# Attention scores kept negated, and the group sums of a Mamba-2 layer issued by matmul form

## The chip, the cores and the metric

The kernel runs on one core of one Trainium2 chip. The metric is the device time of one launch in microseconds (us), the median of several runs. The kernel before was run three times: 1904.80, 1904.31 and 1900.27 us, median 1904.31 us.

## The reference, cut to what matters

One inference step of a small encoder for two request groups that share weights: 512 prompt tokens and 64 sample tokens, 576 token columns in all (`TOK`), everything in fp32. Layer 0 mixes tokens by windowed attention with sinks, layer 1 by a Mamba-2 recurrence (SSD); both also attend to 256 memory tokens and are followed by a squared-ReLU MLP. The change touches two places:

```
def sink_probs(scores, sink):
    m = jnp.maximum(jnp.max(scores, axis=-1, keepdims=True), sink)
    p = jnp.exp(scores - m)
    return p / (jnp.sum(p, axis=-1, keepdims=True) + jnp.exp(sink - m))

# swa_prompt, swa_sample: scores are q.k / 8 + bias, bias = -slope * |distance|
# ssm_mixer, at its end: RMSNorm over each of 8 groups of 192 channels
y = rmsnorm(y.reshape(b, l, SSM_GROUPS, SSM_INNER // SSM_GROUPS), norm_w.reshape(SSM_GROUPS, SSM_INNER // SSM_GROUPS))
```

## The kernel before, in words

Five engines run five instruction streams, tied by semaphores. All large projections stream their weights from HBM as slabs of 128 output features (128 x 1024 floats, 512 KB). A slab passes through SP (load into `raw`, L2139), ACT (`w_hi`, the part that TensorE's fp32r format holds exactly, L471), POOL (`w_lo` = `raw` - `w_hi`, L1941) and TensorE (`eighth`, L917: for each of 8 feature tiles `w_hi`, `w_lo` and `w_hi` again times `big_hi`, `big_hi` and `big_lo`, each in two halves of 288 columns). A ring of four slabs (`RING`) lets the loads run ahead. An eighth is 6 matmul instructions.

**Attention (layer 0).** 24 heads are taken in 12 query tiles of two heads. A tile has five units u0 to u4: u0 the sample's tokens, u1/u2 and u3/u4 the two heads of two pairs of prompt blocks. `attention_steps()` writes out one list of steps that every engine walks: S (scores, PE L1041/L1052), B (`bias_max`, DVE), E (`exps`, ACT), N (`normalise`, DVE), T (transposes on PE, L1065 to L1070, and the copy to `p_t` on ACT, L627 to L631), V (values, PE L1081), O (`take_out`, DVE L1418), K (an eighth of the next query projection on PE) and Q (end of its slab: DVE's L1527/L1529, ACT's `w_hi`). PE fills its time between attention steps with the 8 K of a tile.

`bias_max` (L1554) reads the scores from PSUM, adds the bias, writes `prob` and, through its accumulator, the row maximum with the sink as its start (`stat[..., 0]`), one instruction per head or block, with an accumulator read behind each. It then waits for its own semaphore `biased` and negates the maxima into `stat[..., 1]` with a small `tensor_scalar` (L1561), which signals `max_done`. ACT's `exps` waits for `max_done`, and computes exp(`prob` - max) with the negated maximum as its bias (L610) and exp(sink - max) (L614, L617). SP's loads of the bias table (L2183) for the tile after next wait for `biased`, and the next slab's load stands behind them in SP's queue.

**SSD (layer 1).** Eight groups are taken in four turns of two groups (`PAIRS`; a turn is one pass of `turn`, driven by `ssd_steps`). Each turn runs K eighths of the next tiles' projections between the steps A, seg, off, st, diag, acc for five blocks; near its end come Q (gate with `zs`, DVE L1905; squares `gsq`, ACT L827), G and N. G sums the squares over each group's 192 channels: 1.5 tiles of 128 partitions, so that for group m and column half h one full-height matmul (contraction over 128 rows, L1338) and one half-height matmul (64 rows, L1339; rows 0 to 63 for m = 0, rows 64 to 127 for m = 1) with a matrix of ones accumulate into PSUM bank 4 + 2m + h. ACT's G then takes ln and exp of all four banks (L832, L835), and DVE's N multiplies `mix` by the result (L1911). The last 10 eighths of a turn stand behind G on PE, except that the steps walk on with N between them; the next turn begins with 16 more eighths. Behind its G part ACT has a table load and the next tile's tanh (L779), for which DVE's `silu` (L1791) waits; DVE's `slab_end` (L1418, L1769, L1784) makes the next tiles, and POOL copies their tails (L2042) and then makes a `w_lo`. `alone(pe)` (L449) is a semaphore increment on a semaphore that nobody waits for.

The code quoted above the printed functions is all that the words can't say:

```
BLOCKS = 5; UNITS_J = 5; TILES = 12; RING = 4; KT = 8
fill(eighths - 10); steps.append(("G", 0)); fill(eighths - 6); steps.append(("N", 0)); fill(eighths)
```

## Time and profile before

| what | value |
|---|---|
| runs | 1904.80, 1904.31, 1900.27 us; median 1904.31 us |
| the profiled execution, its own time | 1899.76 us |
| its span in the trace | 1898.0 us, 31359 instructions |
| granted TensorE clock over the span | 0.992 of full speed |
| busy share: PE, PE loads, DVE, ACT, POOL | 95%, 90%, 45%, 34%, 42% |
| HBM traffic | 76 GB/s over the span |

The profile is of one execution. "PE" is TensorE's matmuls, "PEld" its weight loads, which overlap matmuls. An fp32 matmul shows as two entries of PE and two of PEld, an fp32r one as one. A "wait" is idle time of an engine before an instruction, put down to whatever ended last before it; "issue" is idle time that no other instruction explains. The chain of waits is followed back from the last instruction. The attention stage lies between 134 and 303 us of the span, the four turns between 942 and 1317 us.

### The profile page before, as it was taken

What the parts mean: (1) busy time and instruction counts of PE and PEld (TensorE: products, weight loads), DVE (VectorE), ACT (ScalarE), POOL (GpSimd) and SP (SyncE); (2) the same over time, 40 slices, a digit from 0 to 9 for tenths busy, and PEclk for the clock granted to TensorE, in tenths of its full rate; (3) what the DMA queues carried; (4) which work ended last, traced back from release to release, by engine and by line L of the source; (5) the groups of instructions that cost most, each with busy time, mean ns of one, the idle gap of its engine ahead of it and who ended that gap; (6) DMA issues with size and microseconds to landing.
All of it is one profiled execution on the core that took longest, in us unless ns stands there. A gap on an engine that the chain in (4) does not pass through costs nothing.

```text
span 1898.0 us, 31359 instructions
## 1 busy us (share of the span) xinstructions
PE 1799.6 (95%) x13177; PEld 1705.3 (90%) x13177; DVE 853.1 (45%) x1649; ACT 640.7 (34%) x1148; POOL 793.1 (42%) x478
## 2 busy tenths in 40 slices
PE   6998998999999999998999999998999999999996
PEld 6997876998999999998888888787799899999996
DVE  6337887316312121138867676764613611212124
ACT  6326665325222121225323342332623412222221
POOL 1331210333646363541465665755133645545451
PEclk9999999999999999999899999999999999999998
DMA  6521110221222222221212111112022222222221
GB/s 230 181 67 57 62 62 30 67 90 65 81 79 84 83 79 89 78 88 61 67 38 66 59 54 60 45 65 99 23 84 73 72 85 78 90 78 87 80 79 72
DMA packets 42076, 146.57 MB, mean 77 GB/s; under 512 B 4816, under 2 KB 6480, under 8 KB 41680
## 3 DMA queue, kind: packets, MB, share of 16 engines
q1 hardware_dynamic: 40144, 140.59, 21.8%
q10 hardware_dynamic: 1792, 3.97, 0.6%
q8 instruction: 105, 1.72, 0.4%
q14 instruction: 35, 0.29, 0.0%
HBM read 138.13 MB, written 6.41 MB: 76 GB/s over the span
## 4 chain that ended last, share of the span: by engine, by line
PE 79%; DVE 13%; issue 3%; ACT 3%; POOL 1%; DMA 1%; SPq 0%; DVEq 0%; ACTq 0%; POOLq 0%
PE ps L917 66%; DVE u L1784 3%; PE ps L1287 1%; DVE mix L1427 1%; PE ps L900 1%; DVE x L1430 1%; PE ps L1052 1%; PE ps L1070 1%; DVE xp L1418 1%; PE ps L1156 1%; DVE prob L1554 1%; PE ps L1133 1%; DVE big_lo L1371 1%; DMA raw<-in_slabs 1%; PE ps L1081 1%
## 5 line engine op out<-in xcount | busy, mean ns | idle before, releaser
L1941 POOL TENSOR_TENSOR w_lo<-raw,w_hi 128x1024 fp32r<-128x1024 f32 x225 | 555.7, 2472 | 751.1 <-ACT w_hi L471 658.9
L917 PE MATMUL ps<-big_hi,w_hi 128*128 128x288 f32 x3552 | 786.4, 302 | 11.0 <-POOL w_lo L1941 3.1
L917 PE MATMUL ps<-big_hi,w_lo 128*128 128x288 f32 x3552 | 767.0, 297 | 0.0
L917 PE MATMUL ps<-big_lo,w_hi 128*128 128x288 f32 x3552 | 759.7, 297 | 7.5 <-DVE big_lo L1371 7.5
L917 PEld LDWEIGHTS ps<-big_hi,w_hi 128*128 128x128 f32 x3552 | 574.7, 189 | 22.5 <-issue 16.3
L917 PEld LDWEIGHTS ps<-big_lo,w_hi 128*128 128x128 f32 x3552 | 571.9, 189 | 12.8 <-DVE big_lo L1371 11.9
L917 PEld LDWEIGHTS ps<-big_hi,w_lo 128*128 128x128 f32 x3552 | 576.0, 189 | 0.1
L471 ACT ACTIVATE w_hi<-raw 128x1024 fp32r<-128x1024 f32 x242 | 255.2, 1056 | 480.1 <-DMA raw<-in_slabs 479.9
L1683 DVE TENSOR_TENSOR mix<-ps,mix 128x576 f32<-128x576 f32 x62 | 46.9, 757 | 306.3 <-PE ps L917 306.3
L1671 DVE SCALAR_TENSOR_TENSOR relu<-ps,rstd 128x576 f32<-128x576 f32 x60 | 45.4, 756 | 280.2 <-PE ps L917 280.2
L1984 POOL TENSOR_TENSOR hid<-relu 128x576 f32<-128x576 f32 x64 | 98.7, 1544 | 158.7 <-DVE relu L1671 158.5
L1784 DVE SCALAR_TENSOR_TENSOR u<-xp,cpar,u 128x579 f32<-128x579 f32 x84 | 108.6, 1293 | 8.4 <-ACT u L765 6.4
L713 ACT ACTIVATE big_hi<-relu 128x576 fp32r<-128x576 f32 x64 | 43.9, 686 | 157.1 <-DVE relu L1671 155.5
L1369 DVE TENSOR_TENSOR big_lo<-hid,big_hi 128x576 fp32r<-128x576 f32 x64 | 75.6, 1181 | 11.1 <-POOL hid L1984 11.1
L1407 DVE TENSOR_TENSOR sq_sum<-sq_sum,sq 128x576 f32<-128x576 f32 x20 | 16.2, 809 | 114.1 <-ACT sq L490 113.8
L2042 POOL COPY tails<-xp 128x3 f32<-128x3 f32 x56 | 16.0, 315 | 102.3 <-DVE xp L1769 97.1
L821 ACT ACTIVATE dec<-ps 128x384 f32<-128x384 f32 (+1 forms) x40 | 16.1, 455 | 121.1 <-PE ps L1287 121.1
L610 ACT ACTIVATE prob<-prob,stat 128x256 f32<-128x256 f32 (+2 forms) x108 | 50.5, 470 | 9.9 <-DVE stat L1561 9.8
L1554 DVE CUSTOM_DVE_ANT_0 prob<-ps,bias,par 128x128 f32<-128x128 f32 (+2 forms) x120 | 49.2, 440 | 8.2 <-PE ps L1052 7.9
L1418 DVE TENSOR_SCALAR mix<-ps 128x384 f32<-128x384 f32 (+5 forms) x62 | 33.4, 539 | 43.0 <-PE ps L1325 19.0
L917 PE MATMUL ps<-m_hi,w_hi 128*128 128x256 f32 x128 | 38.6, 302 | 14.2 <-POOL w_lo L1941 10.9
L1874 DVE TENSOR_TENSOR dec<-dec,cbm 128x768 f32<-128x768 f32 (+1 forms) x20 | 28.2, 1411 | 51.7 <-ACT dec L821 51.7
(200 smaller groups left out, 1744.8 us busy)
## 6 DMA issues: line engine op xcount, KB each, us to landing
raw<-in_slabs SPq DMA_DIRECT2D x242, 512.0 KB, 3.4
bias<-in_alibi SPq DMA_DIRECT2D x12, 256.0 KB, 2.7
x<-in_x SPq DMA_DIRECT2D x2, 1152.0 KB, 8.3
out_h<-state ACTq DMA_DIRECT2D x4, 384.0 KB, 2.6
out_y<-x SPq DMA_DIRECT2D x2, 576.0 KB, 2.8
kms<-in_mk SPq DMA_DIRECT2D x2, 512.0 KB, 5.1
vms<-in_mv SPq DMA_DIRECT2D x2, 512.0 KB, 6.1
out_y<-x SPq DMA_DIRECT2D x1, 864.0 KB, 3.5
```

The source lines that it names most:

```text
L471: act.activation(w_hi[:, s % RING], raw[:, s % RING], ACT.Copy).then_inc(hi_done, 1)
L610: act.activation(ap, ap, ACT.Exp, bias=stat[:, r, 1, b:b + 1], accum_out=stat[:, r, 2, b:b + 1])
L713: act.activation(big_hi[:, m], relu[:, m % 2], ACT.Square).then_inc(act_hi, 1)
L917: ins = pe.matmul(ps[:, bank + h, 0:hi_c - lo_c], w[:, s % RING, kt], a[:, k0 + kt, lo_c:hi_c], start=start, stop=stop, skip_group_check=True)
L1369: ins = dve.tensor_tensor(dst, src, hi.bitcast(F32), ALU.subtract)
L1418: return dve.tensor_scalar(dst, src, 1.0, None, ALU.mult)
L1554: ins = dve.tensor_tensor_reduce(prob[half, r, k, c0:c1], ps[half, bank, k * 2 * P + c0:k * 2 * P + c1], bias[half, j, e, c0 + d:c1 + d], 1.0,
L1671: dve.scalar_tensor_tensor(out=halves(relu[:, m % 2]), in0=src, scalar=0.0, in1=halves(rstd[:, 1]), op0=ALU.max, op1=ALU.mult).then_inc(fr ...
L1683: dve.tensor_tensor(halves(mix[:, m]), src, halves(mix[:, m]), ALU.add).then_inc(freed, 1)
L1784: dve.scalar_tensor_tensor(out=u[:, t], in0=xp[:, t % 2, j:j + UC], scalar=cpar[:, t, j:j + 1], in1=u[:, t], op0=ALU.mult, op1=ALU.add).th ...
L1941: pool.tensor_tensor(w_lo[:, s % RING], raw[:, s % RING], w_hi[:, s % RING].bitcast(F32), ALU.subtract).then_inc(lo_done, 1)
L1984: pool.tensor_tensor(hid[:, m % 2], relu[:, m % 2], relu[:, m % 2], ALU.mult).then_inc(hid_done, 1)
```

## The change

The attention scores are stored negated: `tensor_tensor_reduce` now has a factor of -1.0 and takes the minimum, started from a negated sink (`minus_sink`, made once by a `tensor_scalar` of 24 columns before the first query tile). The minimum is already the negated maximum, so L1561 and DVE's wait before it go, ACT waits for `biased` instead of `max_done`, and its exponentials take `scale=-1.0` on `prob` and none on `stat`. The memory attention keeps `max_done`, whose count is now `UNITS` lower. In G the four full-height matmuls are issued first, then the four half-height ones with the row half alternating; one `alone(pe)` stands in front of all instead of four. Functions and lines after the edit are one to four lines further down (L917 is L918, L1554 is L1558).

```diff
--- before.py
+++ after.py
@@ -253,6 +253,7 @@
         par = main.take("par", [P, N_PAR])
         mats = main.take("mats", [P, 4, P])
         eps = main.take("eps", [P, 1])
+        minus_sink = main.take("minus_sink", [P, 2 * TILES])
 
         main.p = (main.p + 31) // 32 * 32
         big_start = main.p
@@ -601,20 +602,20 @@
 
                 n_, q, u = n.n + t, t // UNITS_J, t % UNITS_J
                 r, sink = n_ % 4, C_SINK + 2 * q + (u - 1) % 2
-                act.wait_ge(max_done, n_ + 1)
+                act.wait_ge(biased, n_ + 1)
                 if u == 0:
                     parts = [(0, prob[:, r, 0, 0:DEC + P])]
                 else:
                     parts = [(b, prob[:, r, b, P if u < 3 and b == 0 else 0:2 * P]) for b in range(2)]
                 for b, ap in parts:
-                    act.activation(ap, ap, ACT.Exp, bias=stat[:, r, 1, b:b + 1], accum_out=stat[:, r, 2, b:b + 1])
+                    act.activation(ap, ap, ACT.Exp, bias=stat[:, r, 0, b:b + 1], scale=-1.0, accum_out=stat[:, r, 2, b:b + 1])
                 if u == 0:
                     for e in range(2):
                         half = slice(e * DEC, (e + 1) * DEC)
-                        ins = act.activation(stat[half, r, 3, 0:1], stat[half, r, 0, 0:1], ACT.Exp, scale=-1.0,
+                        ins = act.activation(stat[half, r, 3, 0:1], stat[half, r, 0, 0:1], ACT.Exp,
                                              bias=par[half, C_SINK + 2 * q + e:C_SINK + 2 * q + e + 1])
                 else:
-                    ins = act.activation(stat[:, r, 3, :], stat[:, r, 0, :], ACT.Exp, scale=-1.0, bias=par[:, sink:sink + 1])
+                    ins = act.activation(stat[:, r, 3, :], stat[:, r, 0, :], ACT.Exp, bias=par[:, sink:sink + 1])
                 ins.then_inc(exp_done, 1)
 
             def copy_t(t):
@@ -649,7 +650,7 @@
 
                 def exps(c):
                     n_, u = n.n + c, c % 3
-                    act.wait_ge(max_done, n_ + 1)
+                    act.wait_ge(max_done, n_ + 1 - UNITS)
                     rows = P if u else DEC
                     for b in range(2 if u else 1):
                         ins = act.activation(prob[0:rows, n_ % 4, b], ps[0:rows, S_BANK + n_ % 2, b * N_MEM:(b + 1) * N_MEM],
@@ -1329,14 +1330,16 @@
                         pe.wait_ge(gsq_done, at(loop, gsq_done, 1))
                         pe.wait_ge(state_done, at(loop, state_done, BLOCKS))
 
+                        alone(pe)
                         for m in range(2):
                             for h in range(2):
-                                c0, c1 = h * HALF, (h + 1) * HALF
-                                o = ps[:, 4 + 2 * m + h, 0:HALF]
-                                r0 = m * HD
-                                alone(pe)
-                                pe.matmul(o, mats[:, 1], gsq[:, 2 * m, c0:c1], start=True, stop=False)
-                                ins = pe.matmul(o, mats[r0:r0 + HD, 1], gsq[r0:r0 + HD, 1, c0:c1], start=False, stop=True)
+                                pe.matmul(ps[:, 4 + 2 * m + h, 0:HALF], mats[:, 1], gsq[:, 2 * m, h * HALF:(h + 1) * HALF],
+                                          start=True, stop=False)
+                        for h in range(2):
+                            for m in range(2):
+                                half = slice(m * HD, (m + 1) * HD)
+                                ins = pe.matmul(ps[:, 4 + 2 * m + h, 0:HALF], mats[half, 1], gsq[half, 1, h * HALF:(h + 1) * HALF],
+                                                start=False, stop=True)
                         ins.then_inc(gsum_done, 1)
 
             loop.per = SSM_PER
@@ -1530,6 +1533,7 @@
                                          in1=halves(rstd[:, 1]), op0=ALU.mult, op1=ALU.mult).then_inc(freed, 1)
 
             dve.wait_ge(stored, 16 * 4)
+            dve.tensor_scalar(minus_sink[:], par[:, C_SINK:C_SINK + 2 * TILES], -1.0, None, ALU.mult)
             own.mark(dve.memset(q_s[:], 0.0))
             own.wait(loop)
             for j in range(QT):
@@ -1550,15 +1554,12 @@
                         half, e, k, c0, c1, d = slice(b * DEC, (b + 1) * DEC), b, 0, 0, P + DEC, b * DEC
                     else:
                         half, e, k, c0, c1, d = slice(0, P), (u - 1) % 2, b, P if u < 3 and b == 0 else 0, 2 * P, 0
-                    sink = C_SINK + 2 * q + e
+                    sink = 2 * q + e
                     ins = dve.tensor_tensor_reduce(prob[half, r, k, c0:c1], ps[half, bank, k * 2 * P + c0:k * 2 * P + c1],
-                                                   bias[half, j, e, c0 + d:c1 + d], 1.0,
-                                                   par[half, sink:sink + 1], ALU.add, ALU.max,
+                                                   bias[half, j, e, c0 + d:c1 + d], -1.0,
+                                                   minus_sink[half, sink:sink + 1], ALU.add, ALU.min,
                                                    stat[half, r, 0, k:k + 1])
                 ins.then_inc(biased, 1)
-                sums = 2 if u else 1
-                dve.wait_ge(biased, n_ + 1)
-                dve.tensor_scalar(stat[:, r, 1, 0:sums], stat[:, r, 0, 0:sums], -1.0, None, ALU.mult).then_inc(max_done, 1)
 
             def normalise(n_, rows, parts, sink=True, sums=2):
 
```

On PE the order of G's eight matmuls moves in each of the four turns. Before (`ps` the PSUM banks, `gsq` the squares, `mats` the ones; L917 are the eighths around it; a full-height one is L1338, a half-height one L1339):

```order
L917 MATMUL ps<-big_lo,w_hi 128x288 x2
L1338 MATMUL ps<-gsq,mats 128x288
L1339 MATMUL ps<-gsq,mats 128x288
L1338 MATMUL ps<-gsq,mats 128x288
L1339 MATMUL ps<-gsq,mats 128x288
L1338 MATMUL ps<-gsq,mats 128x288
L1339 MATMUL ps<-gsq,mats 128x288
L1338 MATMUL ps<-gsq,mats 128x288
L1339 MATMUL ps<-gsq,mats 128x288
L917 MATMUL ps<-big_hi,w_hi 128x288 x2
```

And in the change:

```order
L918 MATMUL ps<-big_lo,w_hi 128x288 x2
L1336 MATMUL ps<-gsq,mats 128x288 x4
L1341 MATMUL ps<-gsq,mats 128x288 x4
L918 MATMUL ps<-big_hi,w_hi 128x288 x2
```

The same eight matmuls stand between the same neighbours, with one change of form between them instead of seven.

On DVE the piece around units u1 and u2 of a tile, between the normalisation of u0 and the copy of finished values; before:

```order
L1575 TENSOR_SCALAR prob<-prob,stat 128x192 [waits dve_self]
L1554 ISA prob,stat<-ps,bias,par 128x128 [waits t_done,s_done]
L1554 ISA stat 128x1
L1554 ISA prob,stat<-ps,bias,par 128x256
L1554 ISA stat 128x1
L1561 TENSOR_SCALAR stat<-stat 128x2 [waits biased]
L1554 ISA prob,stat<-ps,bias,par 128x128 [waits t_done,s_done]
L1554 ISA stat 128x1
L1554 ISA prob,stat<-ps,bias,par 128x256
L1554 ISA stat 128x1
```

And in the change:

```order
L1576 TENSOR_SCALAR prob<-prob,stat 128x192 [waits dve_self]
L1558 ISA prob,stat<-ps,bias,minus_sink 128x128 [waits t_done,s_done]
L1558 ISA stat 128x1
L1558 ISA prob,stat<-ps,bias,minus_sink 128x256
L1558 ISA stat 128x1
L1558 ISA prob,stat<-ps,bias,minus_sink 128x128 [waits t_done,s_done]
L1558 ISA stat 128x1
L1558 ISA prob,stat<-ps,bias,minus_sink 128x256
L1558 ISA stat 128x1
L1421 TENSOR_SCALAR mix<-ps 128x512 [waits v_done]
```

Nothing stands between the two units any more, and behind them comes the copy out of PSUM, then the normalisation of u1.

## Rows read from the trace of the kernel before

**Rows 1.** Busy time by stage: attention, turns (us; PE, PEld, DVE, ACT, POOL; clock)

```profile
134.00:303.00 169.00, 157.95 (x1295) 130.94 (x1294) 140.14 (x579) 107.83 (x370) 26.08 (x11) 1.00 0.15 54
942.00:1317.00 375.00, 352.27 (x2488) 313.35 (x2486) 250.62 (x341) 125.89 (x183) 222.14 (x189) 1.00 0.18 60
```

**Rows 2.** Page, the chain that ended last, share of the span by engine

```profile
PE 79%; DVE 13%; issue 3%; ACT 3%; POOL 1%; DMA 1%; SPq 0%; DVEq 0%; ACTq 0%; POOLq 0%
```

**Rows 3.** Waits of PE from 134 to 303 us: total us, times, longest

```profile
PE ps L1065 <- DVE prob L1575: 4.0, 3, 1.8
PE ps L1070 <- DVE prob L1575: 3.5, 7, 1.1
PE ps L1070 <- ACT p_t L631: 2.1, 2, 1.1
PE ps L1052 <- DVE stat L1554: 1.4, 4, 0.5
```

**Rows 4.** The negation and the biased maximum by line (ns min/median/max)

```profile
L1561 DVE TENSOR_SCALAR stat<-stat x60: 153/170/1981, 135.0 to 299.2; 128x2 f32<-128x2 f32 x48, 128x1 f32<-128x1 f32 x12
L1554 DVE CUSTOM_DVE_ANT_0 prob<-ps,bias,par x120: 337/476/485, 134.1 to 298.7; 128x256 f32<-128x256 f32 x72, 64x192 f32<-64x192 f32 x24, 128x128 f32<-128x128 f32 x24
```

**Rows 5.** Timeline, sixth query tile (start, us, engine, line, operation, count, idle before)

```profile
205.99 0.32 DVE L1575 TENSOR_SCALAR prob<-prob,stat 128x192 f32<-128x192 f32 x1
...
207.46 2.38 POOL L1941 TENSOR_TENSOR w_lo<-raw,w_hi 128x1024 fp32r<-128x1024 f32 x1 [11.22 <-ACT w_hi L471]
...
208.14 1.71 DVE L1561 TENSOR_SCALAR stat<-stat 128x2 f32<-128x2 f32 x1
...
210.58 1.13 PE L1052 MATMUL ps<-k_all,q_t 64*128 64x256 f32 x8 [0.28 <-DVE stat L1554]
```

**Rows 6.** Timeline, first query tile: ACT behind the slab load

```profile
146.89 1.06 ACT L471 ACTIVATE w_hi<-raw 128x1024 fp32r<-128x1024 f32 x1 [2.20 <-DMA raw<-in_slabs]
```

**Rows 7.** Timeline, eleventh query tile

```profile
274.81 2.34 POOL L1941 TENSOR_TENSOR w_lo<-raw,w_hi 128x1024 fp32r<-128x1024 f32 x1 [10.72 <-ACT w_hi L471]
274.84 2.44 DVE L1575 TENSOR_SCALAR prob<-prob,stat 128x192 f32<-128x192 f32 x1
```

**Rows 8.** Timeline of PE's loads through G of the first turn

```profile
1022.26 0.30 PEld L1338 LDWEIGHTS ps<-gsq,mats 128*128 128x128 f32 x2 [0.16 <-issue]
...
1022.94 0.29 PEld L1339 LDWEIGHTS ps<-gsq,mats 64*128 64x128 f32 x2 [0.39 <-issue]
...
1027.71 0.30 PEld L917 LDWEIGHTS ps<-big_hi,w_hi 128*128 128x128 f32 x2 [0.38 <-issue]
```

**Rows 9.** Chain of waits, 462 to 466 us: four full-height fp32 matmuls in a row

```profile
463.67 1.95 PE ps L869 x8
```

**Rows 10.** Timeline of PE, memory attention: two full-height matmuls of 256 columns

```profile
1327.27 1.13 PE L1133 MATMUL ps<-km,mix 128*128 128x256 f32 x4
```

**Rows 11.** Timelines of ACT, DVE, POOL and PE behind G, first turn

```profile
1027.82 1.23 ACT L832 ACTIVATE grs<-ps,eps 128x1152 f32<-128x1152 f32 x1 [2.09 <-PE ps L1339]
...
1023.70 2.44 DVE L1791 SCALAR_TENSOR_TENSOR u<-th,u 128x579 f32<-128x579 f32 x1 [2.56 <-ACT th L779]
...
1029.76 0.17 DVE L1418 TENSOR_SCALAR xp<-cpar 128x3 f32<-128x3 f32 x1 [1.17 <-PE ps L917]
...
1033.22 1.07 DVE L1791 SCALAR_TENSOR_TENSOR u<-th,u 128x579 f32<-128x579 f32 x1 [2.50 <-ACT th L779]
...
1031.27 2.41 POOL L1941 TENSOR_TENSOR w_lo<-raw,w_hi 128x1024 fp32r<-128x1024 f32 x1
...
1051.26 0.50 PE L917 MATMUL ps<-big_hi,w_hi 128*128 128x288 f32 x2 [1.57 <-DVE zs L1775]
```

**Rows 12.** Third turn: a piece of the chain, and DVE's first tiles of the next

```profile
1236.11 21.00 PE ps L917 x156
...
1256.35 1.55 DVE L1775 SCALAR_TENSOR_TENSOR zs<-ps,rstd 128x576 f32<-128x576 f32 x2 [0.18 <-DVE skips L1418]
```

**Rows 13.** Timeline of ACT, last turn

```profile
1316.07 1.22 ACT L832 ACTIVATE grs<-ps,eps 128x1152 f32<-128x1152 f32 x1 [3.92 <-PE ps L1339]
```

## The prediction

> **What bounds the kernel now.** I read the busy times by stage first. In both stages that the change touches PE is busy 94% of the time: 157.95 of 169.00 us in attention, 352.27 of 375.00 us in the turns, at the full clock (1.00, the 2.4 GHz level) [rows 1]. The chain that ended last runs 79% through PE and 13% through DVE [rows 2]. So an edit pays where it shortens PE's own stream or a piece where PE stands still, and a saving on DVE or ACT alone pays nothing. A whole-span share doesn't say which, so I took the two places apart.
>
> In attention PE stands still for 169.0 - 157.95 = 11.05 us, and the table of waits accounts for all of it: 4.0 + 3.5 + 2.1 + 1.4 = 11.0 us [rows 3]. That is the ceiling for the first half of the change, whatever DVE saves.
>
> In the turns the matmuls of G are themselves on PE's stream. The loads show the cost of their order: after the first full-height matmul the load of the half-height one comes 0.68 us later and only after 0.39 us of idle time that nothing explains but "issue"; the whole of G lasts from 1022.26 to 1027.71, 5.45 us for eight matmuls, 0.68 us each [rows 8].
>
> **Part 1, the negation.** It removes 60 instructions of L1561 and 60 waits of DVE for its own semaphore, and adds one `tensor_scalar` of 24 columns long before PE's first wait of the stage; that one is covered by the projections and costs nothing (uncovered, some 0.2 us by the median of L1561). The -1.0 factor and the minimum ride in an instruction that exists; ACT's `scale` likewise. I take both at nothing: the same instruction with other constants. The bounds are 0 and, if a minimum cost one L1561's median more per use, 120 x 0.17 us of DVE, most of it beside PE.
>
> The median negation takes 0.170 us [rows 4]; with the wait in front I count 0.2 us per unit, on DVE and, for the first `exps` behind it, on ACT. That is 12 us of DVE, nearly all beside a busy PE. What matters more is the longest, 1.98 us. In the sixth tile POOL's `w_lo` runs from 207.46 to 209.84; the negation starts at 208.14 and takes 1.71 us, to 209.85: it is held until POOL is done. L1554 reads scores from PSUM and is never held, its longest of 120 is 0.485 us [rows 4, 5]. So the second unit's L1554 comes after 209.85, and PE's next scores (L1052, 210.58) wait 0.28 us for it [rows 5]. Without L1561 the two units follow each other and end some 1.6 us earlier, and the wait is gone. Term by term, on PE:
> - L1052 waiting for L1554, four times, 1.4 us [rows 3]: gone, 1.4 us.
> - L1070 waiting for L1575, seven times, 3.5 us [rows 3]. Two of about 1.1 us come behind the copy of a query tile, which itself waits for PE; they stay. Five small ones share 3.5 - 2.2 = 1.3 us. Each is the end of a string B, negation, N on DVE; 0.2 us less each, and the whole in two that follow a held negation: 1.2 us.
> - L1070 waiting for ACT's `p_t`, twice, 2.1 us. `p_t` stands on ACT behind a `w_hi` that waits 2.20 us for its slab [rows 3, 6]; that load stands on SP behind a bias load which waits for `biased` of u4. That comes 0.2 us earlier by one negation: 0.4 us for two.
> - L1065 waiting for L1575, three times, 4.0 us: two (longest 1.8 us) where L1575 itself is held, 2.44 us at 274.84 against a `w_lo` that began at 274.81 [rows 3, 7]. Nothing of the change stands in front of either by more than a tenth of a us, they stay. The third is the stage's first unit: 0.2 us.
>
> Sum 3.2 us, between 0 and 11.
>
> **Part 2, the group sums.** PE issues the same eight matmuls with two changes of form (into and out of the half-height run) in place of eight. A full-height fp32 matmul of 288 columns among its like takes 1.95 / 4 = 0.49 us [rows 9], so a change of form costs 0.68 - 0.49 = 0.19 us. For the half-height ones on alternating row halves: four such of 256 columns (L1052, eight entries) take 1.13 us [rows 5], as much as two full-height ones of 256 columns (L1133, four entries, 1.13 us [rows 10]). So a pair costs what one full-height matmul costs. G becomes 4 x 0.49 + 0.19 + 2 x 0.49 + 0.19 = 3.32 us, 2.13 us less a turn. The removed `alone` increments I take at nothing: the idle time before a full-height load (with one in front) is the same 0.38 to 0.39 us as before a half-height one (without) [rows 8]; bounds 0 and 3 x 0.19 us.
>
> One rule of the Trainium skill speaks against the first four: "TensorE: Matmul & The Clock Gate", Part 3, says that a weight load overlaps a running matmul only when its row group differs. By it the eight loads of the full-height run, 0.15 us each by the 0.30 us of two [rows 8], would come on top, 1.2 us a turn, and G would take 4.5 us. The four in a row of [rows 9] show no such gaps, and the measurement decides.
>
> What a turn gains depends on who is late next.
> - Turns 1 and 2: ACT waits 2.09 us for the sums [rows 11], so ln, exp and the next tanh come up to 2.1 us earlier. But DVE can start its next tile (1029.76) only 1.17 us earlier, when it is free; POOL's `w_lo` (1031.27) follows that tile's tails and moves by the same 1.17 us; and L1791 (1033.22), now ready early, falls under it as its predecessor did at 1023.70 (2.44 us against some 0.75 us unheld). DVE thus gains 1.17 us, and PE, which waits 1.57 us for DVE's first `zs` tile at 1051.26, gains as much [rows 11]: 1.17 us a turn, the rest turns into a longer wait there.
> - Turn 3: the chain runs 21.0 us through PE behind G, with no wait at all, and DVE's first `zs` tile is done (half of 1.55 us after 1256.35) at about 1257.1, as PE ends its eighths and goes on to A's transposes [rows 12]. Between 1.17 and 2.13 us, near the latter since PE is first: 2.0 us.
> - Turn 4: ACT has been free for 3.92 us when the sums come, and N and the memory attention stand behind it [rows 13]: 2.1 us.
>
> Sum 2 x 1.17 + 2.0 + 2.1 = 6.4 us, between 3 and 8.5.
>
> **Total**: 3.2 + 6.4 = 9.6 us, 0.50%. The profiled execution took 1899.76 us (span 1898.0), 4.55 us under the median of 1904.31; against itself the sum gives 1890.2, against the median 1894.7 us. Behind each stage PE runs on without waits that depend on the saved work, so the gain is kept. I forecast **1894.7 us**.
>
> **Rivals.**
> - *The half-height pairs don't overlap.* For it: L1339 alone takes 0.68 us as L1338 does. Against: L1052 against L1133. G is then 8 x 0.49 + 2 x 0.19 = 4.3 us, 1.15 us less a turn; turns 1 and 2 keep about 1.15. Total 3.2 + 4.6 = 7.8: 1896.5 us. Chance 0.12.
> - *The hold moves to the next instruction of DVE.* The instruction held now is not special: L1575 is held in the last tiles. If N of u1 starts before POOL ends (209.84), DVE is freed as late as now, and the 1.4 us and half of the 1.2 us stay. Against it: between them stands a copy of 0.7 us, and N needs exponentials of more than a us that can't start before 209. Then 1.2 + 6.4 = 7.6: 1896.7 us. Chance 0.15. The Trainium skill, "SBUF — State Buffer", who interferes with whom, has this rule: the later of a GpSimd instruction and a VectorE one with two SBUF inputs or in a two-port mode is blocked until the first ends. By it the copy out of PSUM is free and N is not.
> - *The two held L1575 slip in front of POOL.* At 274.84 against 274.81 the race is lost by 0.03 us; a tenth of a us on DVE might win it. Two times 1.7 us more: 13.0 in all, 1891.3 us. Chance 0.15.
> - *The turns absorb it.* DVE, already the last at 1051.26, gives nothing: 3.2 + 0 + 0 + 2 + 2: 1897.1 us. Chance 0.07.
> - *Slower.* In the sixth tile L1575 of u0 ends at 206.31, 1.15 us before POOL's `w_lo` [rows 5]; in the eleventh it loses that race and PE stands 1.7 us. If ACT, relieved of waits, makes `w_hi` over a us earlier in tiles 4 to 10, seven tiles pay 1.74 us each, 12.2 us, and gain nothing of the 3.2 but 1.2: -6.4 - 1.2 + 12.2 = +4.6, 1908.9 us. Against: `w_hi` stands on ACT behind `p_t` copies whose time PE sets. It decides from about 1.1 us of shift. Chance 0.03.
>
> **How the numbers follow.** Forecast 0.48, the rivals as given. A measurement of this kernel can tell about 0.3%, 5.7 us. The runs before spread over 4.5 us, which adds to every case: the range 1886.5 to 1901.5 us takes in the best case less the spread below the median, and above it half of each part's gain failing (1899.5) and a little of the spread. Faster by over 0.3%: most of the forecast, two thirds of the smaller ones, 0.78; within 0.3% 0.18; slower 0.04.
>
> **What would show it.** L1561 gone and no entry of DVE over 1 us in tiles 4 to 10; PE's idle time in the attention stage down from 11.0 to about 8 us, L1052's waits gone; G at 3.3 us, with idle loads only at its two changes of form; ACT's ln in turns 1 and 2 without a wait worth naming; the wait for `zs` in turns 1 and 2 up from 1.57 to about 2.5 us. G at 4.3 us refutes the pairing, an L1575 or `tensor_tensor` of 1 to 2 us in the middle tiles refutes the end of the hold, and a first wait of the next turn that grows by the full 2.1 us would mean the turns absorb it.

## The result, and the profile after

The changed kernel ran in 1888.85 us (median of 5 runs, 1883.80 to 1890.73) against 1903.85 us for the kernel before on the same chip (5 runs, 1900.27 to 1904.80): ratio 0.9923, 95% interval 0.9905 to 0.9941, 15.0 us less where 9.6 were forecast. The profiled execution took 1888.85 us, its span 1887.0 us (before: 1899.76 and 1898.0).

Two single executions differ in more than the change, so I first matched PE's streams: the same matmul in both traces, and by how much it comes earlier. Between 132.7 and 299 us (times of before) the distance grows by 3.9 us, through the four turns by 7.4 us. The rest is not work of the edited lines: the trace after is 2.1 us late at the start of the K projection, where its granted clock stayed at the lower level longer, and wins 1.4 us behind 1356 us, where the clock of the one before fell to it for some 3 us and that of this one did not. Another 0.3 us come between the two stages. -3.9 - 7.4 - 1.4 - 0.3 + 2.1 = -10.9 of the 11.0 us.

Busy time by stage, the two stages of [rows 1] (PE, PEld, DVE, ACT, POOL, clock):

```profile
134.00:300.00 166.00, 157.60 (x1300) 131.17 (x1299) 123.67 (x521) 106.23 (x370) 27.72 (x12) 1.00 0.16 55
935.00:1308.00 373.00, 348.13 (x2528) 316.60 (x2528) 256.18 (x344) 127.18 (x185) 223.10 (x190) 1.00 0.18 61
```

PE's idle time in attention fell from 11.05 to 8.4 us. Its table of waits, to be held against [rows 3] (all lines are one to four higher now: L1554 is L1558, L1575 is L1576, L1052 is L1053):

```profile
PE ps L1066 <- DVE prob L1576: 3.9, 3, 1.8
PE ps L1071 <- DVE prob L1576: 2.2, 2, 1.1
PE ps L1071 <- ACT p_t L632: 2.0, 2, 1.1
```

The row of scores waiting for the biased maximum is gone, as are the five small waits of L1071, and no entry of DVE in tiles 4 to 10 lasts over 1 us. The held normalisation of the eleventh tile stands, [rows 7]:

```profile
273.29 2.50 DVE L1576 TENSOR_SCALAR prob<-prob,stat 128x192 f32<-128x192 f32 x1
273.33 2.34 POOL L1942 TENSOR_TENSOR w_lo<-raw,w_hi 128x1024 fp32r<-128x1024 f32 x1 [10.25 <-ACT w_hi L472]
```

DVE is now first by 0.04 us, where it had been second by 0.03, and is held all the same: 2.50 us where an unheld one takes 0.32 [rows 5]. The trace before had shown this already, in the twelfth tile:

```profile
289.96 2.50 DVE L1575 TENSOR_SCALAR prob<-prob,stat 128x192 f32<-128x192 f32 x1
290.00 2.35 POOL L1941 TENSOR_TENSOR w_lo<-raw,w_hi 128x1024 fp32r<-128x1024 f32 x1 [12.84 <-ACT w_hi L471]
```

In all the traces of this case this normalisation starts 0.03 to 0.04 us ahead of `w_lo` 19 times, and it is held each time. The profile gives GpSimd's times only roughly, so which of the two is truly first can't be told.

G in the third turn, from the chain of waits; 3.35 us in place of 5.45 [rows 8], and the same 21 us of PE behind it as in [rows 12]:

```profile
1225.51 2.18 PE ps L1336 x8
1227.69 1.17 PE ps L1341 x8
1228.86 20.98 PE ps L918 x156
```

Behind G of the first turn, timelines of ACT, DVE and PE; they answer to [rows 11]:

```profile
1023.61 1.23 ACT L833 ACTIVATE grs<-ps,eps 128x1152 f32<-128x1152 f32 x1
...
1044.32 2.33 DVE L1421 TENSOR_SCALAR skips<-par 128x6 f32<-128x6 f32 x1
1046.83 1.42 DVE L1776 SCALAR_TENSOR_TENSOR zs<-ps,rstd 128x576 f32<-128x576 f32 x2 [0.18 <-DVE skips L1421]
...
1047.74 0.50 PE L918 MATMUL ps<-big_hi,w_hi 128*128 128x288 f32 x2 [2.34 <-DVE zs L1776]
```

ACT finds the sums ready (it waited 2.09 us for them), and PE now waits 2.34 us for the first `zs` where it waited 1.57: of the 2.1 us that G became shorter, 0.8 went into this wait. A tiny instruction stands in front of that `zs`: `skips`, 6 elements, takes 2.33 us beside a `w_lo` that began at 1044.25.

### The profile page after: what moved, and what is told of

The parts are those of the page before. It is cut to its first block, busy times and chain, and to the rows that moved or that the text cites. A ratio compares the mean times of both kernels' runs of the same rounds, so it can differ in the third digit from the quotient of the medians.

```text
span 1887.0 us, 31288 instructions
## 1 busy us (share of the span) xinstructions
PE 1788.9 (95%) x13177; PEld 1702.6 (90%) x13177; DVE 837.0 (44%) x1590; ACT 639.2 (34%) x1148; POOL 791.9 (42%) x478
## 4 chain that ended last, share of the span: by engine, by line
PE 78%; DVE 13%; ACT 4%; issue 3%; POOL 1%; DMA 1%; SPq 0%; DVEq 0%; ACTq 0%; POOLq 0%
PE ps L918 66%; DVE u L1785 3%; PE ps L1288 1%; DVE mix L1430 1%; PE ps L901 1%; PE ps L1082 1%; PE ps L1053 1%; DVE x L1433 1%; PE ps L1071 1%; DVE xp L1421 1%; PE ps L1157 1%; PE ps L1134 1%; DVE big_lo L1374 1%; DMA raw<-in_slabs 1%; ACT u L766 1%
## 5 line engine op out<-in xcount | busy, mean ns | idle before, releaser
L918 PE MATMUL ps<-big_hi,w_hi 128*128 128x288 f32 x3552 | 783.6, 301 | 12.5 <-DVE zs L1776 4.7
L918 PE MATMUL ps<-big_lo,w_hi 128*128 128x288 f32 x3552 | 757.1, 297 | 7.7 <-DVE big_lo L1374 7.7
L918 PE MATMUL ps<-big_hi,w_lo 128*128 128x288 f32 x3552 | 763.3, 296 | 0.0
L918 PEld LDWEIGHTS ps<-big_hi,w_hi 128*128 128x128 f32 x3552 | 573.0, 189 | 24.1 <-issue 17.8
L918 PEld LDWEIGHTS ps<-big_lo,w_hi 128*128 128x128 f32 x3552 | 569.4, 189 | 13.1 <-DVE big_lo L1374 12.1
L918 PEld LDWEIGHTS ps<-big_hi,w_lo 128*128 128x128 f32 x3552 | 573.8, 189 | 0.1
L1558 DVE CUSTOM_DVE_ANT_0 prob<-ps,bias,minus_sink 128x128 f32<-128x128 f32 (+2 forms) x120 | 48.4, 440 | 13.7 <-PE ps L1053 11.8
L918 PE MATMUL ps<-m_hi,w_hi 128*128 128x256 f32 x128 | 39.7, 310 | 14.4 <-POOL w_lo L1942 11.1
```

What stands on the lines that cost most here:

```text
L918: ins = pe.matmul(ps[:, bank + h, 0:hi_c - lo_c], w[:, s % RING, kt], a[:, k0 + kt, lo_c:hi_c], start=start, stop=stop, skip_group_check=True)
L1558: ins = dve.tensor_tensor_reduce(prob[half, r, k, c0:c1], ps[half, bank, k * 2 * P + c0:k * 2 * P + c1], bias[half, j, e, c0 + d:c1 + d], ...
```

## The experiments

Twelve kernels ran. Every one carries a profile; those with several runs also a ratio to the kernel before on the same chip.

### neg_only and sums_only: each half alone

`neg_only` is the changed kernel with G's loop as in the diff's removed lines; `sums_only` is the kernel before with the added ones.

> The changed kernel with the matmuls of G in their old order: the negation's half alone. If the two halves add as in the prediction, the attention stage is as in the changed kernel: PE's entries from the stage's start to its end in 3.9 us less than before, no entry of DVE over 1 us in tiles 4 to 10, and G lasts its old 5.45 us in each turn, so 3 to 5 us less than before in all (ratio 0.997 to 0.9985). Rival: the turns also gained by the negation (max_done is no longer raised there, the waits are other ones); then G is 5.45 us and the turns still come out over 1 us shorter than before.

> The kernel before with G's matmuls in the new order: the second half alone. Theory: G lasts 3.3 us in place of 5.45, turns 1 and 2 gain 1.5 us each, turn 3 2.2, turn 4 2.1, 7.4 us in all (ratio about 0.996), and the attention stage keeps its 11 us of PE idle time and L1561 its hold of 1.7 to 2.0 us. Rival: part of the 15 us between the medians stands in neither half but in how the two fall together; then neg_only and sums_only gain clearly less in sum than the changed kernel does.

`neg_only`: 1890.84 us (6 runs, 1884.31 to 1896.81), ratio 0.9939 (0.9918 to 0.9960). `sums_only`: 1895.66 us (5 runs), ratio 0.9964 (0.9951 to 0.9977). The traces say what the theory says: `neg_only` gains 4.0 us in attention, its waits there are those of the changed kernel, and G keeps its old pace (two rows of the chain, one matmul each):

```profile
1226.24 0.71 PE ps L1339 x2
1226.95 0.68 PE ps L1340 x2
```

Its four turns still gain 0.4 us together. That is not the negation: `before_shifted` below, the kernel before with nothing but its tiles moved, has the same turns.

The time of `neg_only` does not agree: 11 us less, where its trace accounts for 4.4 in the two places. And its six runs lie in two clumps, 1884.3 to 1887.3 and 1894.4 to 1896.8. Its profile is one of the quick ones, and the matched streams show where: between 1488 and 1879 us, in one unbroken stretch of PE without a wait in it, it gains 9.5 us. That is taken up below.

`sums_only` shows the second surprise. I read how long each turn lasts from one G to the next, by the start of G's first matmul in PE's timelines (before: 1022.29, 1126.46, 1230.62 and 1310.62 us):

| kernel | turn 1 | turn 2 | turn 3 | wait for `zs` in turns 1 and 2 |
|---|---|---|---|---|
| before | 104.17 | 104.16 | 80.00 | 1.6 |
| neg_only | 104.04 | 104.05 | 79.88 | 1.6 |
| changed | 102.69 | 102.66 | 77.81 | 2.3 |
| sums_only | 104.38 | 102.76 | 77.90 | 2.3 |
| same_half | 102.66 | 104.28 | 77.79 | 2.3 |
| before_shifted | 104.05 | 104.06 | 79.90 | 1.6 |
| after_unshifted | 104.36 | 102.77 | 77.90 | 2.3 |

The column "turn 1" lasts from the first G to the second. Of turns 1 and 2 each gains 1.4 to 1.5 us or nothing, with the same waits. Where the tiles lie as in the kernel before (`sums_only`, `after_unshifted`) it is 1.4 us; the other 0.1 us comes with the moved tiles alone. The windows of `sums_only` behind its wait for `zs` (the number before the last two is the granted clock):

```profile
1052.00:1054.00 2.00, 0.09 (x1) 0.12 (x2) 1.82 (x3) 0.20 (x1) 1.62 (x2) 1.00 0.60 223
1054.00:1056.00 2.00, 2.00 (x11) 1.98 (x12) 1.71 (x4) 1.43 (x3) 0.94 (x2) 0.64 0.03 8
1056.00:1058.00 2.00, 2.00 (x11) 2.00 (x10) 0.75 (x2) 0.89 (x2) 2.00 (x3) 0.50 0.00 0
```

and the same place in the changed kernel:

```profile
1046.00:1048.00 2.00, 0.26 (x2) 0.29 (x3) 1.82 (x3) 0.38 (x1) 1.44 (x2) 1.00 0.56 219
1048.00:1050.00 2.00, 2.00 (x19) 2.00 (x18) 1.74 (x5) 1.46 (x4) 1.11 (x2) 1.00 0.00 0
1050.00:1052.00 2.00, 2.00 (x19) 2.00 (x18) 0.96 (x4) 1.27 (x3) 2.00 (x3) 1.00 0.03 8
```

PE stood still as long in both; in one execution the clock then fell to the 1.2 GHz level for some 3 us, 11 matmuls in 2 us in place of 19, and the turn's gain was gone (a turn with the fall is 1.6 us longer than one without).

### same_half: is it the alternation?

```
-                        for h in range(2):
-                            for m in range(2):
+                        for m in range(2):
+                            for h in range(2):
                                 half = slice(m * HD, (m + 1) * HD)
```

> The changed kernel with the four half-height matmuls of G in the order h inside m, so that two in a row use the same half of the rows. If alternating halves are what lets two of them overlap, the half-height run takes 4 x 0.49 us in place of 2 x 0.49 for its starts, and G about 4.3 us in place of 3.35, 0.7 to 1.0 us more a turn. If not (a half-height matmul is cheap as such, or only the changes of form cost), G stays at 3.3 to 3.4 us.

One run, 1885.01 us (its last stretch is a quick one too, by 9.5 us). G from its chain:

```profile
1228.46 2.17 PE ps L1336 x8
1230.62 1.18 PE ps L1341 x8
```

3.35 us again, to the hundredth: the order in which the row halves are issued does nothing. That does not say that the pairs don't overlap. The eight entries of the half-height run don't start one after the other in either kernel, but two at a time. A window of a tenth of a us shows the first pair, and in the changed kernel I add the second:

```profile
1227.62 0.51 PE L1341 MATMUL ps<-gsq,mats 64*128 64x288 f32 x2
1227.96 0.41 PE L1341 MATMUL ps<-gsq,mats 64*128 64x288 f32 x2
```

and in `same_half`:

```profile
1230.55 0.52 PE L1341 MATMUL ps<-gsq,mats 64*128 64x288 f32 x2
```

The two starts of a pair lie 0.01 us apart, four pairs in a row, in both orders. In the kernel before nothing starts in pairs, each entry comes 0.34 us behind the one before it:

```profile
1230.94 0.41 PE L1338 MATMUL ps<-gsq,mats 128*128 128x288 f32 x1
1231.28 0.51 PE L1339 MATMUL ps<-gsq,mats 64*128 64x288 f32 x1
```

Are half-height matmuls cheap as such? The kernel before has a place that answers: L1308 of a turn's first block runs two half-height matmuls in a row, both on rows 0 to 63, and two full-height ones of the same 192 columns in the next block:

```profile
960.18 0.91 PE L1308 MATMUL ps<-sq,btok 64*128 64x192 f32 x4
970.51 0.81 PE L1308 MATMUL ps<-sq,btok 128*128 128x192 f32 x4
```

From entry to entry it is 0.16 us in both, with no pairs; the 0.1 us more is the first step behind a change of form. So a half-height matmul costs what a full-height one costs when its neighbours use the same rows, and half of that when they use the other rows. In `same_half` the pairs must then be one of each half, out of the order of issue; the trace doesn't name the rows of an entry, so this last step is argued.

### old_order_one_alone: the increments

```
+                        alone(pe)
                         for m in range(2):
                             for h in range(2):
                                 c0, c1 = h * HALF, (h + 1) * HALF
                                 o = ps[:, 4 + 2 * m + h, 0:HALF]
                                 r0 = m * HD
-                                alone(pe)
                                 pe.matmul(o, mats[:, 1], gsq[:, 2 * m, c0:c1], start=True, stop=False)
```

The other lines are the changed kernel's, with the matmuls interleaved as before.

> The matmuls of G interleaved as in the kernel before, with one increment of alone(pe) in front of the eight in place of four. If the changes of form are the cost, G stays at 5.4 to 5.5 us and the turns are as long as before. If the increments cost something, G is shorter: by up to 3 x 0.19 = 0.57 us (4.9 us), which would leave that much less to the order.

One run, 1895.45 us. Entries of 0.68 us as in the kernel before, and the same G of 5.4 us:

```profile
1227.79 0.68 PE ps L1340 x2
1228.47 0.68 PE ps L1339 x2
```

The three increments cost nothing. By PE's timelines G takes 5.42 us from its first matmul to the next eighth here and before, and 3.28 to 3.29 us in the first three turns of every kernel with the new order, 2.14 us less. The steps from one entry's start to the next say where they come from. Among full-height entries a step is 0.24 us, two to a matmul, as in [rows 9]. Around a change of form two steps are 0.34 us, the one into the new form and the one behind it: 0.19 to 0.20 us for a change. From pair to pair of the half-height run it is again 0.24 to 0.25 us. Six changes less at 0.19 are 1.1 us, and four half-height matmuls that share their time two by two are 2 x 0.49 = 1.0 us less than four that stand alone. Together that is the 2.1 us, and it fits both totals: 8 x 0.49 + 8 x 0.19 = 5.44, and 6 x 0.49 + 2 x 0.19 = 3.32.

### neg_kept_unread and neg_by_column: DVE's hold, DVE's string, or ACT

```
                 ins.then_inc(biased, 1)
+                sums = 2 if u else 1
+                dve.wait_ge(biased, n_ + 1)
+                dve.tensor_scalar(stat[:, r, 1, 0:sums], stat[:, r, 0, 0:sums], -1.0, None, ALU.mult)
```

That is `neg_kept_unread`, on top of the changed kernel. `neg_by_column` is the kernel before with

```
-                dve.tensor_scalar(stat[:, r, 1, 0:sums], stat[:, r, 0, 0:sums], -1.0, None, ALU.mult).then_inc(max_done, 1)
+                for k in range(sums):
+                    ins = dve.tensor_scalar(stat[:, r, 1, k:k + 1], stat[:, r, 0, k:k + 1], -1.0, None, ALU.mult)
+                ins.then_inc(max_done, 1)
```

> The changed kernel with the negation and the wait in front of it put back on DVE, while ACT goes on reading the negated maxima of the first instruction, so that the result of the added one is read by nobody. It parts DVE's time from ACT's. If the gain of the attention stage comes from DVE no longer standing behind POOL's w_lo, the added instruction is held for 1.7 to 2.0 us in tiles 4 to 10 again, PE's waits for it are back (1.4 us of L1053 <- DVE) and the stage is 2 to 3.9 us longer than in the changed kernel (165.1 us from the stage's start in the changed kernel's trace against 169.0 before). Rival: the gain is ACT's shorter wait (exps a negation earlier); then the stage keeps at least 3 of its 3.9 us although the instruction is back. From the other clock drops and the last stretch's rate of an execution, neither reads anything; the stage alone is compared.

> The kernel before with the negation of two maxima written as two instructions of one column each (96 more instructions would be 108 in place of 60). In the kernel before every held negation had two columns, and none of the 12 with one column fell beside a w_lo, so the trace does not tell whether the form matters. If it is the two-column form that is held behind POOL, none of the single-column ones takes over 0.3 us, the waits of L1052 for L1554 (1.4 us) go and attention is 1 to 2.5 us shorter than before, with an L1575 or tensor_tensor no more held than in the changed kernel. If any instruction of DVE between two SBUF operands is held, the first of the two takes 1.7 us as before and attention is as long as before or up to 0.5 us longer. The Trainium skill, "VectorE: DVE Perf Modes", says that a single-source instruction takes the mode with both port pairs when its outermost dimension over one is even or equal in source and result; a row of one element has no such dimension, so by it the first case is to be expected.

The instruction whose result nobody reads, by its line, and PE's waits in attention (one run, 1893.99 us):

```profile
L1565 DVE TENSOR_SCALAR stat<-stat x60: 153/169/2239, 135.3 to 302.4; 128x2 f32<-128x2 f32 x48, 128x1 f32<-128x1 f32 x12
```

```profile
PE ps L1066 <- DVE prob L1579: 3.8, 3, 1.8
PE ps L1071 <- DVE prob L1579: 3.7, 7, 1.1
PE ps L1071 <- ACT p_t L632: 2.4, 2, 1.3
PE ps L1053 <- DVE stat L1558: 1.3, 4, 0.3
```

It is held for 1.7 to 2.2 us in tiles 4 to 10, and all that the change had removed is back: 1.3 us of L1053, the five small waits of L1071. The matched streams put the stage 2.9 us behind the kernel before, and 6.7 behind the changed one, more than expected; the clock fell twice in it (0.58 in 164 to 168 us, 0.79 and 0.78 in 292 to 300). `sums_only`, whose attention is that of the kernel before, came out 1.4 us later across one such fall, between 164 and 166 us of before. Across its own two falls `neg_kept_unread` comes out 1.8 and 1.5 us later, 3.3 of the 6.7 us; without them the stage would be as long as before, within 0.4 us. What is left of the rival, ACT's shorter wait, is at most 0.1 us: [rows 3] 2.1, changed kernel 2.0, `after_again` (below) 2.3.

The same two views of `neg_by_column` (one run, 1897.51 us):

```profile
L1562 DVE TENSOR_SCALAR stat<-stat x108: 142/153/155, 135.3 to 299.2; 128x1 f32<-128x1 f32 x108
```

```profile
PE ps L1065 <- DVE prob L1577: 4.1, 3, 1.8
PE ps L1070 <- DVE prob L1577: 3.7, 7, 1.1
PE ps L1070 <- ACT p_t L631: 2.2, 2, 1.1
```

The longest of 108 takes 155 ns, though `w_lo` runs beside them as before (208.88 to 211.27 us in the sixth tile). So for this instruction the form decides: two columns are held, one is not. The Trainium skill, "VectorE: DVE Perf Modes", "What auto-detection actually checks", says that an instruction with one source, out of and into SBUF, takes the mode with both ports when its outermost dimension over one is even or equal in source and result, and a single column has no such dimension. The trace agrees: 1.98 us for the longest with two columns [rows 4], 0.155 with one. One column does not protect every instruction: the `tensor_tensor` of one column in `normalise` (L1569 before), which has two sources in SBUF, takes 1.02 us at 149.39 in the trace before, and ends with the `w_lo` beside it.

Together the two kernels part the terms. L1052's 1.4 us hang on the hold: gone here, back there. The small waits of L1070 hang on the extra instruction in DVE's string, held or not: 3.7 us, 7 times, in both. The stage of `neg_by_column` is only 0.4 us shorter than before, with one fall of the clock (0.57 at 164 us) in it, across which it comes out 1.4 us later. Apart from that fall the hold is worth 1.9 us to the stage, about half of what the whole negation is worth.

### wlo_behind_both and after_again: the holds that the change left

```
+            FIRST_Q = 2 * MEM_SLABS + KV_SLABS + QT + 2
...
+                slab = s + (loop.i or 0) * loop.per.get("hi_done", 0)
+                if 0 < slab - FIRST_Q < TILES:
+                    pool.wait_ge(normed, UNITS_J * (slab - FIRST_Q) + 1)
                 pool.wait_ge(hi_done, at(loop, hi_done, s + 1))
...
+                pool.wait_ge(cur_done, at(loop, cur_done, 1))
                 for kind, b in ssd_steps(last):
```

The first three stand in POOL's `split_lo`, the last in its `turn`. `after_again` is the changed kernel unaltered.

> The changed kernel, with two waits on POOL: in attention a w_lo starts only behind the first normalisation of its tile, and in each turn of the mixer only behind DVE's prelude (heads_cur, cpar, skips). What is tested is that the holds that the change left are worth their length to PE: L1576 of tiles 11 and 12 (2.50 us against 0.35, PE waits of 1.77 us each) and skips in turns 1 and 2 (2.33 us in place of 0.16, in front of zs, for which PE waits 2.3 us each time). Theory: the two waits of 1.77 us shrink below 0.5, the waits for zs from 2.3 to under 0.7 us, and nothing else waits longer: 3.5 + 3.5 = 5 to 7 us less than the changed kernel, 1882 to 1884 us (ratio to the kernel before about 0.989), and no drop of the granted clock behind zs. Rival: POOL runs behind, w_lo comes late for PE (L918 <- POOL w_lo, 1.6 us now in one place) or its tails move later, and the sum is nothing or worse.

> The changed kernel once more, beside wlo_behind_both on one chip. Two things that differ between executions are asked for: whether the granted clock falls to the 1.2 GHz level behind the 2.3 us waits for zs in turns 1 and 2 (it did in sums_only's turn 1 and same_half's turn 2, each time taking back the 1.5 us that the turn had gained, and not in the first profile of the changed kernel), and at which of two rates the last stretch of 390 us runs (302 to 303 matmuls in 40 us in five profiles so far, 310 in neg_only and same_half, worth 9.5 us). If the clock drop is chance behind any wait of 2.3 us, about one turn in three shows it. Time expected: 1884 to 1891 us, median 1888.

`wlo_behind_both`: 1879.41 us (6 runs, 1869.44 to 1884.08), ratio 0.9880 (0.9860 to 0.9900); `after_again` beside it 1888.65 us (6 runs, 1871.50 to 1891.08), ratio 0.9907 (0.9878 to 0.9937). By the medians it is 9 us quicker than the changed kernel; by the profiles the turns gain 3.5 us more and the attention 2.3, with a fall of the clock at 164 us in it. PE's waits from 120 to 300 us, and DVE at the start of turn 1's second half:

```profile
PE ps L1071 <- DVE prob L1576: 2.2, 2, 1.1
PE ps L1071 <- ACT p_t L632: 1.9, 2, 1.0
PE ps L1066 <- DVE prob L1576: 0.3, 1, 0.3
```

```profile
1039.69 0.16 DVE L1421 TENSOR_SCALAR skips<-par 128x6 f32<-128x6 f32 x1
1040.04 0.76 DVE L1776 SCALAR_TENSOR_TENSOR zs<-ps,rstd 128x576 f32<-128x576 f32 x1 [0.18 <-DVE skips L1421]
```

Two waits of 1.77 us are gone, `skips` takes 0.16 us in place of 2.33, and `zs` no longer appears among PE's waits. A turn lasts 100.79 us in place of 102.69. POOL's own lateness costs nothing that I can find. `after_again` lost turn 1's gain to the clock (104.27 us, clock 0.61 at 1048) and kept turn 2's (102.66).

### before_shifted, after_unshifted, before_shifted_32, wlo_both_aligned: where a tile lies

`minus_sink` stands in front of `big_hi` and `big_lo`, PE's moving operands, and pushes them and all behind them up by 96 bytes. `before_shifted` is the kernel before with

```
         eps = main.take("eps", [P, 1])
+        main.take("pad", [P, 2 * TILES])
```

`before_shifted_32` has `[P, 8]` there. `after_unshifted` takes `minus_sink` behind `stat` in the attention's area. `wlo_both_aligned` is `wlo_behind_both` with `big_hi` rounded up to 2048 bytes in place of 32.

> The kernel before, with 24 floats a partition taken between eps and big_hi and used by nothing, so that big_hi, big_lo and every tile behind them lie 96 bytes higher, as they do in the changed kernel, whose minus_sink stands there. Asked: why executions of kernels with minus_sink come out 9 to 18 us under their own median (3 of 6 of neg_only, 2 of 6 of after_again, 1 of 6 of wlo_behind_both, same_half's one; two of these were profiled, and ran the last stretch at 310 matmuls in 40 us in place of 302 to 303), while none of the 27 runs of the kernel before, the 5 of sums_only and the one of neg_by_column did. Theory (place): the rate depends on where the tiles lie; then one to three of the six runs here are 9 us or more under the rest, which stay at 1900 to 1904 us. Rival (instructions): it depends on the streams of DVE and ACT, or is chance; then all six lie within 1899 to 1905 us.

> The changed kernel with minus_sink taken behind stat, at the end of the attention's own area, so that big_hi, big_lo and the rest lie where they do in the kernel before; same instructions otherwise. Theory (place): no run falls 9 us under the others; all six within 1886 to 1893 us. Rival (instructions): one to three of the six are at 1871 to 1884 us as in neg_only and after_again. In either case the chain of the profile shows the attention 3.9 us and the turns up to 7.4 us shorter than before, less 1.5 us for each turn with a clock drop.

> The kernel before with 8 unused floats in place of before_shifted's 24, so that big_hi starts 32 bytes higher: at a multiple of 64 bytes that is not one of 128 (119872), where the kernel before has it 32 bytes past a multiple of 128 (119840) and before_shifted and the changed kernel at a multiple of 128 (119936). In before_shifted 5 of 12 runs were 8 us or more under the other 7 (1880.45 to 1891.77 against 1898.79 to 1904.46), and its profile ran both long stretches of PE at 309 to 310 matmuls in 40 us; after_unshifted had none such in 5, so the place stands as the cause. Open is what of the place. If 64 bytes are enough, runs at 1880 to 1892 us appear here too, about two in five; if it takes 128, all are within 1898 to 1905 us as in the kernel before.

> wlo_behind_both with big_hi at a multiple of 2048 bytes (120832), tiles behind it 896 bytes higher than in the changed kernel. If a coarser alignment makes the quicker rate of the two long stretches (310 matmuls in 40 us) the rule and not the chance, most runs are at 1861 to 1871 us, 18 us under wlo_behind_both's usual 1878 to 1884. If only the multiple of 128 counts, the runs spread as there: most at 1878 to 1884, one or two in six 9 to 18 us lower, median 1875 to 1882, ratio to the kernel before about 0.987.

| kernel | `big_hi` at byte | runs | us | ratio to before |
|---|---|---|---|---|
| before_shifted | 119936 | 12 | 7 at 1898.79 to 1904.46, 4 at 1889.29 to 1891.77, 1 at 1880.45 | 0.9967 (0.9947 to 0.9987) |
| after_unshifted | 119840 | 5 | 1887.97 to 1894.36, median 1891.72 | 0.9947 (0.9934 to 0.9960) |
| before_shifted_32 | 119872 | 5 | 1890.47 to 1893.91, median 1892.51 | 0.9948 (0.9935 to 0.9962) |
| wlo_both_aligned | 120832 | 4 | 1879.85 to 1883.86, median 1882.70 | 0.9896 (0.9882 to 0.9909) |

Windows of 40 us in the two long stretches in which PE has nothing to wait for (PE's share and its matmuls are the second and third figure). The kernel before:

```profile
600.00:640.00 40.00, 40.00 (x302) 40.00 (x302) 8.15 (x8) 8.11 (x8) 18.29 (x9) 1.00 0.24 79
1600.00:1640.00 40.00, 40.00 (x302) 40.00 (x302) 11.19 (x13) 9.80 (x11) 25.06 (x12) 1.00 0.26 85
```

`neg_only`:

```profile
600.00:640.00 40.00, 40.00 (x303) 40.00 (x302) 7.50 (x7) 6.59 (x7) 17.57 (x8) 1.00 0.26 87
1600.00:1640.00 40.00, 40.00 (x310) 40.00 (x309) 9.48 (x10) 9.49 (x10) 22.25 (x11) 1.00 0.25 80
```

`before_shifted`, whose profiled execution is the one of 1880.45 us:

```profile
600.00:640.00 40.00, 40.00 (x310) 40.00 (x309) 8.91 (x9) 7.70 (x8) 18.80 (x8) 1.00 0.25 83
1600.00:1640.00 40.00, 40.00 (x310) 40.00 (x309) 9.94 (x11) 8.43 (x9) 21.92 (x10) 1.00 0.26 93
```

`before_shifted_32`:

```profile
600.00:640.00 40.00, 40.00 (x305) 40.00 (x304) 8.07 (x8) 7.00 (x7) 18.78 (x8) 1.00 0.26 92
1600.00:1640.00 40.00, 40.00 (x305) 40.00 (x304) 10.90 (x12) 9.12 (x10) 23.47 (x11) 1.00 0.23 80
```

The place is the cause: unused bytes alone bring the quick runs to the kernel before, and with `minus_sink` elsewhere none of five runs of the changed one was quick (five runs alone would be weak evidence; none of the 53 of the kernel before, at the same address, was either). With `big_hi` at 119936 a stretch runs at 302 to 303 matmuls in 40 us or at 310, the whole stretch at one of them, and each quick stretch is worth 9.5 us (the matched streams of `before_shifted` gain 9.5 in the first, 9.5 in the second). At 119840 and 120832 all runs stay at 302 to 303 as far as their profiles show, at 119872 the profile has 305 in both stretches, and all five runs lie within 3.4 us of each other, 9.5 us under the kernel before. My two guesses about the rule fell: 64 bytes past a multiple of 128 gives neither the old rate nor the lottery but a third rate, and a coarse alignment gives the slow one. What of the address counts stays open, and so does what decides the draw at 119936. `wlo_behind_both` with `big_hi` at 119872 would be the next to try; it was not run. The move also changes the two stages a little: `before_shifted` gains 0.35 us in attention and 0.1 us in each of turns 1 to 3.

## Why the prediction came out right, step by step

**Attention: 3.2 forecast, 3.9 measured** (3.6 to 4.1 in `neg_only`, `old_order_one_alone` and `after_again`; 3.5 in `after_unshifted`, where the moved tiles add nothing). L1052 for L1554, 1.4 us: gone, and `neg_kept_unread` and `neg_by_column` show that it hung on the hold. L1070 for L1575, 1.2: 3.5 to 2.2, through the shorter string and not through the hold, as `neg_by_column` shows. L1065's two of 1.8: they stayed, and 0.1 us came off the row. ACT's `p_t`, 0.4: 0.1, the term that was too high; why `w_hi` did not come forward by the whole 0.2 us a negation was not followed up. The waits fell by 2.9 us in sum and the stage by 3.9. Of the rest 0.35 us is the place of the tiles; the other 0.6 us lies in PE's entries and not in its idle time, and I had no term for it.

**G: 3.32 forecast, 3.35 measured, for the reason given.** The step "a change of form costs 0.68 - 0.49 = 0.19 us" held: two steps of 0.34 us in place of 0.24. The step "a pair costs what one full-height matmul costs" held too: the entries of the half-height run start two at a time, and a pair takes 0.49 us. The pairs did not hang on the alternating order, though: they form in `same_half` as well, whose first two half-height matmuls use the same rows. That run's expectation knew only two cases, no overlap without alternation or half-height matmuls that are cheap as such, and it was neither. The rival that the pairs don't overlap (4.3 us) fell with it. The increments at nothing: right, by `old_order_one_alone`. The load rule of the Trainium skill, "TensorE: Matmul & The Clock Gate", Part 3, that spoke for 4.5 us did not decide: the eight full-height entries took 2.17 us, 0.2 more than [rows 9] and 1.0 less than by that rule.

**The turns: 6.4 forecast, 7.4 measured in the first profile**, 7.0 of them by the instructions and 0.4 with the place of the tiles, as `neg_only` and `before_shifted` show. Turns 3 and 4: 2.0 and 2.1 forecast, 2.1 each measured in `after_unshifted`. Turns 1 and 2: 1.17 each forecast, 1.4 measured there in turn 2 and 1.5 in the changed kernel, since the L1791 that I had held for 2.4 us was held for 1.77, and the wait for `zs` grew by 0.8 us, not by 0.9. What I had not priced is the clock behind that wait. Of six profiled executions with the 2.3 us wait, twelve turns in all, five turns gained nothing and showed the lower level of the granted clock behind it. Of six with the 1.6 to 1.7 us wait two turns of twelve showed it, both in `before_shifted_32`. Five against two is too few to say that the longer wait makes it likelier. The rival that the turns absorb the gain was right in those five, by a mechanism that it did not name.

**The rivals in attention.** The hold did not move to the next DVE instruction (none over 1 us in tiles 4 to 10), and ACT's `w_hi` did not come a us earlier. The two held L1575 started 0.04 us ahead of `w_lo` and gained nothing. The rival took a lead by a hair for enough, and its rows show only the eleventh tile: the twelfth had that lead before and was held. `wlo_behind_both` shows what they are worth.

**The total: 9.6 forecast, 15.0 between the medians.** The part that comes from the instructions is best read from `after_unshifted`: 1891.72 against 1901.69 us, 10.0 us, with an interval of 7.6 to 12.6. Its trace shows 3.5 us in attention and 5.6 in turns 2 to 4, and nothing in turn 1, where the clock fell; with turn 1's 1.4 it would be 10.5. That agrees with the 9.6, each part a little over its forecast. The other 5 us are outside the sum. The intervals of the two measurements overlap (11.2 to 18.1 for the 15.0), so part of them can be chance. A cause that is shown is the shift by 96 bytes: in 11 runs of the changed kernel 8 lie at 1887.65 to 1891.08 us and 3 at 1871.50 to 1883.80, and the same shift alone took 0.33% off the kernel before on average. I had counted the added tile as one `tensor_scalar` and nothing else. That its address moves PE's two operands was in the diff, but nothing in the trace before could have priced it.

## What to carry to other kernels

A matmul costs what its neighbour makes it cost: group those of one form, and pay for a change of form (0.19 us here) as seldom as the sums allow. Half-height matmuls on different row halves, put next to each other, ran two at a time (0.49 us a pair of 288 columns); on the same rows they ran one by one at the full price, and standing alone between full-height ones they paid it too. Before a price is divided out of two totals, look at the starts of the entries: another pair of prices fits the same totals. A small DVE instruction out of and into SBUF can cost ten times its length where GpSimd works: here a one-source one with two columns, and a `tensor_tensor` even with one; look for entries whose longest is far above their median, and either give them another form or make GpSimd wait for them, if it has time. And before a gain of a few tenths of a per cent is put down to an edit, repeat the kernel with the addresses of before: 96 bytes in front of PE's operands moved this one by a third of a per cent on average, 32 bytes by half a per cent, as much as the edit.

## What the runs showed that I had not expected

- PE's rate at the full granted clock and without a wait has three levels here, 302 to 303, 305 and 310 matmuls of 288 columns in 40 us, by where `big_hi` lies; at one address it differs between executions, and between two stretches of one execution (`neg_only`: 303 and 310).
- A pause of PE of 1.6 to 2.3 us is followed in some executions by some 3 us at the lower clock level, worth 1.4 to 1.6 us, and in others by none. Three such places more or less would make the spread of 4.5 us between the runs of the kernel before; that this is where it comes from was not shown, since each run but one of a kernel has no profile.
- DVE's `tensor_scalar` of 0.32 us that starts 0.04 us ahead of GpSimd's instruction still lasts until that one ends; with a lead of 0.40 us (`wlo_behind_both`) it takes its 0.32 us. What lead is enough was not measured.
- Four half-height fp32 matmuls of G start in pairs 0.01 us apart even when the first two issued use the same rows (`same_half`), though two on the same rows with no others beside them go one by one (L1308, 0.16 us from entry to entry).
